# Two transformer blocks on one core: VectorE's low part of the next unit moved ahead of an eviction, one norm made in one step, one turn moved to TensorE

## The reference

```python
def rms_norm(x, g):
    return x * lax.rsqrt(jnp.mean(x * x, axis=-1, keepdims=True) + NORM_EPS) * g

# end of the first block
u = rms_norm(h, norm_ffn_g[l])
g, up = jnp.split(u @ w_gate_up[l], 2, axis=-1)
h = h + (jax.nn.silu(g) * up) @ w_down[l]
return rms_norm(h, norm_final_g)

# each of the two layers of the second block
h = rmsnorm(x, ffn1_norm[i])
x = x + 0.5 * swiglu(h, ffn1_w_gate[i], ffn1_w_up[i], ffn1_w_down[i])
...                                  # attention over the sequence and a memory
x = x + jnp.concatenate([o_s, o_m], axis=-1) @ w_out[i]
h = rmsnorm(x, ffn2_norm[i])
x = x + 0.5 * swiglu(h, ffn2_w_gate[i], ffn2_w_up[i], ffn2_w_down[i])
```

## Time and profile before

| | |
|---|---|
| median of 3 runs | 1363.41 us |
| the profiled execution, its own time | 1363.44 us |
| its span in the trace | 1361.6 us |
| VectorE busy | 1051.7 us, 77% |
| ScalarE busy | 703.3 us, 52% |
| GpSimd busy | 143.6 us, 11% |
| DMA | 246.30 MB, mean 181 GB/s |
| granted TensorE clock, mean | 1.000 |

### The profile page before, as it was taken

How to read it: one execution, slowest core, us unless ns; L and a number is a source line. 1 busy time by engine, 2 the same in 40 slices (tenths; PEclk the granted TensorE clock), 3 DMA queues, 4 the chain that set the end, 5 groups by cost and what they waited for, 6 DMA issues and landing times.

```text
span 1361.6 us, 18032 instructions
## 1 busy us (share of the span) xinstructions
PE 1344.4 (99%) x6505; PEld 1109.0 (81%) x6505; DVE 1051.7 (77%) x1810; ACT 703.3 (52%) x936; POOL 143.6 (11%) x162
## 2 busy tenths in 40 slices
PE   9999999999999999999999999999999999999999
PEld 7987887888877888887778888788888888788887
DVE  6895678887869778767678888688887888688775
ACT  5556445544454444567654444544445677544442
POOL 4052002000020000142010000100000432100000
PEclk9999999999999999999999999999999999999999
DMA  8644457555544555454346555465555542455552
GB/s 272 198 160 148 158 182 265 200 193 203 201 163 169 198 200 202 168 186 142 122 140 217 197 201 186 127 237 192 185 185 189 182 155 94 160 180 187 200 202 90
DMA packets 108537, 246.30 MB, mean 181 GB/s; under 512 B 4952, under 2 KB 9220, under 8 KB 108352
## 3 DMA queue, kind: packets, MB, share of 16 engines
q1 hardware_dynamic: 106416, 240.19, 52.3%
q0 software_dynamic: 1776, 4.74, 1.1%
q10 hardware_dynamic: 288, 0.61, 0.1%
HBM read 244.45 MB, written 1.07 MB: 180 GB/s over the span
## 4 chain that ended last, share of the span: by engine, by line
PE 95%; DVE 2%; ACT 1%; POOL 0%; issue 0%; DMA 0%; ACTq 0%; POOLq 0%
PE ps L1653 26%; PE ps L1603 17%; PE ps L1605 16%; PE ps L1604 16%; PE ps L1658 13%; PE ps L1843 1%; DVE wlo L983 1%; PE ps L1629 1%; PE ps L1881 1%; PE ps L1897 1%; PE ps L2162 1%; DVE xx L1028 0%; ACT xx L661 0%; DMA gcol<-in_gcol 0%; DVE sc L1176 0%
## 5 line engine op out<-in xcount | busy, mean ns | idle before, releaser
L1653 PE MATMUL ps<-whi,xx 128*128 128x512 f32 x1600 | 378.9, 389 | 0.0
L1653 PEld LDWEIGHTS ps<-whi,xx 128*128 128x128 f32 x1600 | 300.3, 188 | 62.3
L988 DVE TENSOR_TENSOR wlo<-raw,whi 128x2048 fp32r<-128x2048 f32 x120 | 274.8, 2290 | 66.5 <-ACT whi L632 65.1
L632 ACT ACTIVATE whi<-raw 128x2048 fp32r<-128x2048 f32 x120 | 229.1, 1909 | 90.7 <-PE ps L1658 90.7
L1176 DVE STREAM_TRANSPOSE sc<-sc 32x128 f32<-32x128 f32 x800 | 242.2, 303 | 11.9
L624 ACT ACTIVATE whi<-raw 128x2048 fp32r<-128x2048 f32 (+1 forms) x135 | 204.7, 1530 | 82.7 <-PE ps L1605 53.9
L1603 PE MATMUL ps<-whi,hhi 128*128 128x512 f32 x504 | 198.6, 394 | 1.7 <-DVE hlo L1181 1.7
L983 DVE TENSOR_TENSOR wlo<-raw,whi 128x2048 fp32r<-128x2048 f32 x75 | 171.3, 2289 | 36.9 <-ACT whi L624 36.5
L1658 PE MATMUL ps<-wlo,xx 128*128 128x512 f32 x800 | 197.6, 389 | 0.0
L1603 PE MATMUL ps<-whi,xx 128*128 128x512 f32 x464 | 188.5, 406 | 8.8 <-DVE wlo L983 8.6
L1605 PE MATMUL ps<-whi,hlo 128*128 128x512 f32 x504 | 196.5, 390 | 0.0
(11 more groups left out here) (277 smaller groups left out, 1289.6 us busy)
## 6 DMA issues: line engine op xcount, KB each, us to landing
raw<-in_ffn_gate_up SPq DMA_DIRECT2D x88, 1024.0 KB, 5.2
raw<-in_ffn_w_down SPq DMA_DIRECT2D x44, 1024.0 KB, 5.0
raw<-in_w_in SPq DMA_DIRECT2D x40, 1024.0 KB, 5.1
raw<-in_gate_up SPq DMA_DIRECT2D x22, 1024.0 KB, 5.2
raw<-in_w_out SPq DMA_DIRECT2D x12, 1024.0 KB, 4.9
raw<-in_w_down SPq DMA_DIRECT2D x11, 1024.0 KB, 5.0
raw<-in_w_mem_kv SPq DMA_DIRECT2D x4, 1024.0 KB, 5.2
raw<-in_w_in SPq DMA_DIRECT2D x4, 512.0 KB, 6.9
```

The source lines that it names most:

```text
L632: act.activation(whi[:, c % 3, :], raw[:, c % 3, :], ACT.Copy).then_inc(hi_done, 1)
L988: dve.tensor_tensor(wlo[:, c % 3, :], raw[:, c % 3, :], whi[:, c % 3, :], ALU.subtract)\
L1653: pe.matmul(ps[:, banks[r], :], x(4 * half + k, P * r, P)[part], whi[:, slot, 512 * k:512 * k + 512], start=half == 0 and k == 0 and part ...
```

## The change

1. In `boundary` VectorE runs `lo(u + 1)` before the upper half of `turned_gain` and no longer after it. This holds for all five boundaries.
2. At the boundary before f = 1 VectorE adds the sums of the second norm for both tiles in one instruction (`first_sums`, put behind `lo(u + 2)`), and GpSimd takes one power over both tiles instead of two pairs of instructions.
3. In step 0 of f = 1 the turn is made by TensorE, in the middle of the matmuls of unit u0+3, into PSUM bank 2. ScalarE and VectorE then read PSUM in place of `hidT`. The counts of the semaphores follow (`last_turn`).

```diff
@@ norm, GpSimd
-                    pool.wait_ge(pool_ms, c + 1)
+                    pool.wait_ge(pool_ms, c + 1 if c < place(N_F1, 0) else c + 1 - RT)
@@ GpSimd, L == 0
                     norm(N_FIN)
-                    norm(N_F1)
+                    c = place(N_F1, 0)
+                    pool.wait_ge(first_ms, 1)
+                    pool.tensor_tensor(rstd[:, c:c + RT], ms[:, c:c + RT], mhalf[:, :].to_broadcast([P, RT]), ALU.pow)\
+                        .then_inc(rstd_ready, RT)
                     row_scale(N_F1, 0.5)
@@ ffn, ScalarE
-                hidden_hi(j0, 0)
+                if f == 1:
+                    act.wait_ge(h_ps, last_turn(f) - 1)
+                    act.activation(hhi[:, 0, :], ps[:, 2, :], ACT.Copy).then_inc(h_hi, 1)
+                else:
+                    hidden_hi(j0, 0)
@@ boundary, VectorE
+                lo(u + 1)
                 turned_gain(T, n, 1)
-                lo(u + 1)
                 if n == N_F1:
                     dve.wait_ge(tr_ps, turns_of(T) + 4)
                     for r in range(RT):
                         scaled(N_FIN, res, res, r)
                 lo(u + 2)
+                if n == N_F1:
+                    first_sums()
+
+            def first_sums():
+
+                c = place(N_F1, 0)
+                dve.wait_ge(sq_done, 2 * c + 2 * RT)
+                both = ss[:, 2 * c:2 * c + 2 * RT].rearrange("p (r h) -> p r h", h=2)
+                dve.scalar_tensor_tensor(out=ms[:, c:c + RT], in0=both[:, :, 0], scalar=EPS, in1=both[:, :, 1],
+                                         op0=ALU.add, op1=ALU.add).then_inc(first_ms, 1)
@@ ffn, VectorE
                 hidden(j0, gate_banks(0))
-                turn(j0)
+                if f != 1:
+                    turn(j0)
                 lo(u0 + 4)
-                hidden_lo(j0, 0, hidT)
+                hidden_lo(j0, 0, ps[:, 2, :] if f == 1 else hidT)
@@ gate_up_half, TensorE
-            def gate_up_half(u, slot, half, banks):
+            def gate_up_half(u, slot, half, banks, between=None):
                 pe.wait_ge(hi_done, u + 1)
                 for r in range(RT):
+                    if r == 1 and between:
+                        between()
@@ ffn, TensorE
-                gate_up_half(u0 + 3, (u0 + 3) % 3, 1, gate_banks(1))
+                gate_up_half(u0 + 3, (u0 + 3) % 3, 1, gate_banks(1), (lambda: turn_hidden(j0, 2)) if f == 1 else None)
```

More of the change, by code:

```diff
@@ L317, in row_factor, with last_turn @@
             return rstd[:, c:c + 1]
+        def last_turn(f):
+            return f + 1 if f < 1 else f + 2
         def gate_banks(J):
@@ L350, in build @@
         frs_ready, first_tile = sem("frs_ready"), sem("first_tile")
+        first_ms = sem("first_ms")
         silu_done, h_mul, h_hi, h_ready = sem("silu_done"), sem("h_mul"), sem("h_hi"), sem("h_ready")
@@ L720, in hidden_hi @@
                 def hidden_hi(J, par):
-                    act.wait_ge(h_turned, J - f + 1)
+                    act.wait_ge(h_turned, J - last_turn(f) + 2)
                     act.activation(hhi[:, par, :], hidT, ACT.Copy).then_inc(h_hi, 1)
@@ L747, in ffn @@
                 silu(j0 + 10, gate_banks(10), u0 + 30)
-                act.wait_ge(h_ps, f + 1)
+                act.wait_ge(h_ps, last_turn(f))
                 act.activation(hhi[:, 0, :], ps[:, 0, :], ACT.Copy).then_inc(h_hi, 1)
@@ L1662, in gate_up_half, with turn_hidden @@
                 ins.then_inc(unit_used, 1)
-            def turn_hidden(J, f):
+            def turn_hidden(J, bank):
                 pe.wait_ge(h_mul, 2 * J + 2)
                 for n in range(4):
-                    ins = pe.transpose(ps[:, 0, P * n:P * n + P], hid[:, P * n:P * n + P], ident)
+                    ins = pe.transpose(ps[:, bank, P * n:P * n + P], hid[:, P * n:P * n + P], ident)
                 ins.then_inc(h_ps, 1)
@@ L1779, in between @@
                 def between():
-                    turn_hidden(j0 + 10, f)
+                    turn_hidden(j0 + 10, 0)
                 if f in (1, 3):
```

## The result

The changed kernel takes 1354.38 us (median of 6 runs, 1353.86 to 1355.55), the kernel before 1363.26 us (median of 6 runs beside them, 1362.51 to 1363.78). The ratio is 0.9937, with a 95% interval from 0.9927 to 0.9948: 8.9 us or 0.65% faster. The forecast was 11.4 us faster, 1352.1, with a range to 1354.2. The direction was right; 2.5 us of the gain are missing.

The account below looks back on a forecast made before the run. TensorE, busy 99% of the span, was taken as the bound. Five boundary waits (-9.85), the `hlo` wait (-1.96) and four added transposes (+0.44) sum to -11.37 us, giving 1352.1; range 1351.3 to 1354.2.

Parts of the forecast that it names:

- What bounds the kernel, and the price of a wait: TensorE, busy 99% of the span, bounds the kernel; each of its six equal waits costs 1.97 us, not 1.71.
- The low part before f = 1: Moved into VectorE's 2.70 us gap it runs 390.4 to 392.7, leaves `xx` at 393.04 untouched, removes the wait: -1.97 us.
- Before f = 2 and 4: Gap too short: first `xx` 0.86 late, yet each boundary wait goes (-1.97 us); slack before the first down matmul falls to nothing.
- The turn on TensorE: Step 0 of f = 1: wait for `hlo` removed, -1.96 us; four transposes added, +0.44, running on time.
- The norm in one step: Before f = 1: silu 1.6 to 3.8 us earlier, but hidden behind TensorE's matmuls of u0+2: worth 0.
- the later bound: GpSimd's factor before f = 1 is there only at 404.5, held behind the 2.28 us of `lo(u0+3)`; otherwise 402.3.
- The low part before f = 0: Boundary before f = 0: same shape as before f = 1, so the same value, -1.97 us; earlier transfers cost nothing.
- (b): A new wait at the first down unit (f = 2 and 4, or f = 1) replaces an old one: 1354 to 1356; 13 in 100.
- (c): The waits only move: TensorE reaches u0+2 earlier and waits there instead, 1363.4 us; 4 in 100.
- (d): Slower: transposes in TensorE's queue wait for a late hidden product in f = 1, 1367.4 us; 3 in 100.
- nothing over 0.3 us: Sign of success: after the start, TensorE's list of waits holds none above 0.3 us.
- wrong would be: Signs of failure: idle before L1693 or the first down matmul, low parts longer beside other work, matmuls over 0.227 us apart.

Follow-up runs that it names:

- The change with the loads spread: The changed kernel with GpSimd's four loads started apart, after the low parts of u0+3, u0+9, u0+12 and u0+17 of f = 0: 1351.74 us.
- loads started with u0+5: The changed kernel with GpSimd's four loads held until the low part of u0+2 is done, as the transfer of u0+5 is: 1352.43 us.
- before, loads sooner: The kernel before with GpSimd's factor for later moved behind the start of its four loads, nothing else changed: 1364.05 us, ratio 1.0007.

## Why the prediction missed, point by point

**What bounds the kernel, and the price of a wait: right.** For each wait that went away 1.97 us were forecast. Where nothing else changed, the part behind the boundary is shorter by 1.97 to 2.01 (f = 2, 3 and 4 in the table of the result).

**The low part before f = 1: right.** It ran 390.57 to 392.86 in the gap, the first `xx` followed at 393.23, and TensorE had no idle time before unit u0+1.

**Before f = 2 and 4: right, and as close as forecast.** The first `xx` comes 692.38 - 688.77 = 3.61 after the last residual piece, before 694.87 - 692.12 = 2.75: 0.86 late, the number of the prediction. In the changed kernel `hlo` ends at 709.99 and the first down matmul starts at 710.11, with 0.43 in place of 0.39 for its length. VectorE's timeline of this place, which answers to the earlier trace rows:

```profile
688.77 0.68 DVE L1078 SCALAR_TENSOR_TENSOR res<-ps,res 128x512 f32<-128x512 f32 x1
690.17 2.29 DVE L995 TENSOR_TENSOR wlo<-raw,whi 128x2048 fp32r<-128x2048 f32 x1 [0.72 <-ACT whi L632]
692.38 0.87 DVE L1040 SCALAR_TENSOR_TENSOR xx<-ps,gcol,xx 128x256 fp32r<-128x256 f32 x2
...
702.01 5.05 DVE L1198 STREAM_TRANSPOSE sc<-sc 32x128 f32<-32x128 f32 x16
```

**The turn on TensorE: right.** Its timeline, answering to the earlier trace rows: between the start at 406.39 and that at 410.49 lie 16 matmuls and the four transposes, 4.10 - 16 x 0.227 = 0.47 for the 0.44 of the forecast, and no idle before them:

```profile
406.39 1.98 PE L1678 MATMUL ps<-whi,xx 128*128 128x512 f32 x8
408.21 0.60 PE L1693 MATMUL ps<-cst,sc 128*128 128x128 f32 x4
408.56 2.09 PE L1678 MATMUL ps<-whi,xx 128*128 128x512 f32 x8
410.49 1.98 PE L1683 MATMUL ps<-wlo,xx 128*128 128x512 f32 x8
```

**The norm in one step: the sum right (0), one wait misread.** I let silu wait for GpSimd's last instruction, the factor. It needs only the product ahead of it (`act.wait_ge(frs_ready, 2)` in the kernel). So the factor, which ran beside `lo(u0+3)` for 2.15 us as the later bound had it, held nothing up:

```profile
402.22 2.15 POOL L493 TENSOR_SCALAR small<-small 128x2 f32<-128x2 f32 x1
```

Silu started at 402.52, 0.39 after the end of the product (401.93 and 0.20 long).

**The low part before f = 0: the step that failed.** The prediction said that the boundaries before f = 0 and 3 "have the same shape (VectorE idle 2.7 between the same two instructions) and I take the same value", and of transfers that "TensorE waits for no transfer after the start, so this is worth nothing, and costs nothing". The shape on VectorE is the same. But f = 0 is the one boundary behind which GpSimd has four loads in its queue, 4.2 MB, behind two instructions that low parts had held up. I had both facts in hand: the `ms` of 1.57 us beside a `wlo`, and the Trainium skill (SBUF — State Buffer, Who interferes with whom), by which VectorE with two SBUF inputs and GpSimd reading SBUF exclude each other. I used them only at f = 1, for the norm, where nothing hangs on them. The trace agrees with that rule here: `ms` took 1.56 us beside a low part and 0.30 without, the factor 1.81 and 0.26. At f = 0 they would have said that GpSimd's loads start sooner (2.80 by the traces, counted from the residual piece), and the question "what does a faster engine start, and with what does that collide" was asked of SyncE alone. The measured term is +0.80 there in place of -1.97 (the wait was won, and 2.8 us were lost one step later); the other terms give 9.50 where 9.40 was forecast. That TensorE waits for no transfer was true of its list of waits and no bound: ScalarE did wait, 2.84 us for u0+6, in that very step of the kernel before, and there the cover was already thin:

```profile
225.50 1.91 ACT L624 ACTIVATE whi<-raw 128x2048 fp32r<-128x2048 f32 x1
233.12 1.92 ACT L624 ACTIVATE whi<-raw 128x2048 fp32r<-128x2048 f32 x1 [2.84 <-DMA raw<-in_gate_up]
```

**The rivals.** (b), a new wait at the first down unit, came nearest in size (1354 to 1356 was its price), but that is luck: neither its place nor its cause was what happened. (c) and (d) did not come: TensorE did not wait at u0+2, and the transposes had no idle before them. No rival held a term for a transfer. The range is also drawn otherwise than the prediction says: the far half of (b) begins at 1355, while 1354.2 leaves room for one wait back (1354.07) and no more. Of the signs, "nothing over 0.3 us" in TensorE's list was broken (1.0 and 0.7); none of those listed under "wrong would be" came, since none is about step 1 of f = 0.

**A better version.** The change with the loads spread is 2.6 us faster than the change as made: 1351.74 against 1354.38, where the kernel before, timed beside each, took 1363.05 and 1363.26. The norm edit can be left out of it.

## What to carry to other kernels

When an instruction is moved out of the way of another engine, ask what that engine does next, down to the transfers in its queue; here loads that started 2.8 us sooner cost 2.8 us, more than the 1.97 of the wait that was removed. Same-looking places in a program are priced one by one, for every engine's queue and not only for the one that is edited. A list of TensorE's waits tells what it costs now; the waits of the engines that feed it tell how much cover is left.

## What the runs showed of the hardware

With the DMA engines full, the order in which transfers started decided which one was late; the bytes were the same. With 4.2 MB of GpSimd's loads started 0.1 us after it or 0.15 us before it, the 1 MB weight transfer of u0+5 landed in 5.3 us (loads started with u0+5) and 6.8 us (kernel before). With the loads 2.05 and 2.97 us ahead it took 15.7 us (before, loads sooner) and 15.5 us (the change). The next transfer (u0+6), started about 2 us later, took 14.9, 15.0, 18.4 and 15.8 us in these four. An estimate: the four loads and the two transfers are 6.3 MB, and from 216 to 228 the two traces of before and after moved 361 to 413 GB/s, which makes 15 to 17 us for all of it, close to what the transfers behind took. How the DMA engines divided the time between loads and transfers no run here shows.
